# Expert stage of a mixture layer turned around: expert weights as the stationary operand, 96 token slots streaming past them

## The reference, cut to what matters

```python
logits = (h @ w_router).astype(jnp.float32)
top_val, top_idx = lax.top_k(logits, TOP_K)
top_w = jax.nn.softmax(top_val, axis=-1)
...
for e in range(N_EXPERTS):
    out = out + combine[..., e:e + 1] * _swiglu(h, w_gate[e], w_up[e], w_down[e])
```

## Time and profile before

| | |
|---|---|
| median of 3 runs | 1530.99 us (1530.94 to 2025.26) |
| profiled execution, first to last instruction | 1530.3 us |
| expert stage in it, from the first gather | 528.4 us to about 1520 us |
| one job | 123.2 us |
| PE, PEld busy | 1485.2 us (97%), 1268.3 us (83%) |
| DVE, ACT busy | 1154.3 us (75%), 1007.7 us (66%) |
| moved by DMA | 430.75 MB |

### The profile page before, as it was taken

How to read it: one execution, slowest core, us unless ns; L and a number is a source line. 1 busy time by engine, 2 the same in 40 slices (tenths; PEclk the granted TensorE clock), 3 DMA queues, 4 the chain that set the end, 5 groups by cost and what they waited for, 6 DMA issues and landing times.

```text
span 1530.3 us, 20635 instructions
## 1 busy us (share of the span) xinstructions
PE 1485.2 (97%) x7842; PEld 1268.3 (83%) x7842; DVE 1154.3 (75%) x872; ACT 1007.7 (66%) x834; POOL 15.5 (1%) x44
## 2 busy tenths in 40 slices
PE   5999999999999799999999999999999999999997
PEld 5898899997898688888888888888888888888775
DVE  4356644445456689888888888989889988888996
ACT  4568543344568477767767767777777777776775
POOL 3000000000000000000000000000000000000000
PEclk9999999999999899999999999999999999999998
DMA  9433455554433389999999989999999998998993
GB/s 342 139 115 109 165 180 179 178 192 154 149 125 111 124 305 372 370 326 376 377 319 373 373 323 373 375 336 355 373 370 326 375 374 317 375 376 320 351 368 119
DMA packets 185376, 430.75 MB, mean 281 GB/s; under 512 B 9048, under 2 KB 11096, under 8 KB 185328
## 3 DMA queue, kind: packets, MB, share of 16 engines
q1 hardware_dynamic: 181920, 426.27, 77.7%
q0 software_dynamic: 1184, 3.22, 0.7%
q10 hardware_dynamic: 2224, 0.59, 0.2%
HBM read 429.01 MB, written 1.05 MB: 281 GB/s over the span
## 4 chain that ended last, share of the span: by engine, by line
PE 89%; ACT 4%; DVE 3%; issue 2%; DMA 1%; ACTq 0%; DVEq 0%
PE ps L1264 81%; PE ps L1605 2%; PE ps L1635 2%; DMA wif<-in_w_in_dram 1%; ACT whi L454 1%; DVE wlo L835 1%; ACT L464 1%; PE ps L1411 1%; PE ps L1283 1%; DVE y L857 0%; PE ps L1672 0%; PE ps L1670 0%; PE ps L1424 0%; DVE y L1022 0%; ACT qkc L626 0%
## 5 line engine op out<-in xcount | busy, mean ns | idle before, releaser
L835 DVE TENSOR_TENSOR wlo<-raw,whi 128x2048 fp32r<-128x2048 f32 x405 | 926.4, 2291 | 294.3 <-ACT whi L454 293.9
L454 ACT ACTIVATE whi<-raw 128x2048 fp32r<-128x2048 f32 x405 | 776.8, 1919 | 409.2 <-PE ps L1264 408.3
L1264 PE MATMUL ps<-whi,xT_hi 128*128 128x512 f32 x1056 | 418.7, 397 | 1.5 <-DVE wlo L835 1.5
L1264 PE MATMUL ps<-wlo,xT_hi 128*128 128x512 f32 x1056 | 412.6, 391 | 0.0
L1264 PE MATMUL ps<-whi,xT_lo 128*128 128x512 f32 x1056 | 411.7, 390 | 0.0
L1264 PEld LDWEIGHTS ps<-wlo,xT_hi 128*128 128x128 f32 x1056 | 198.4, 188 | 42.5
L1264 PEld LDWEIGHTS ps<-whi,xT_hi 128*128 128x128 f32 x1056 | 198.9, 188 | 41.1 <-issue 1.7
L1264 PEld LDWEIGHTS ps<-whi,xT_lo 128*128 128x128 f32 x1056 | 199.1, 188 | 39.3
L1264 PE MATMUL ps<-whi,hid_hi 128*128 128x512 f32 (+1 forms) x536 | 210.9, 393 | 0.7 <-DVE hid_lo L1150 0.7
L1264 PE MATMUL ps<-wlo,hid_hi 128*128 128x512 f32 (+1 forms) x536 | 208.7, 389 | 0.0
L1264 PE MATMUL ps<-whi,hid_lo 128*128 128x512 f32 (+1 forms) x536 | 208.7, 389 | 0.0
(11 more groups left out here) (218 smaller groups left out, 854.9 us busy)
## 6 DMA issues: line engine op xcount, KB each, us to landing
raw<-in_moe_w_gate_dram SPq DMA_DIRECT2D x112, 1024.0 KB, 5.1
raw<-in_moe_w_up_dram SPq DMA_DIRECT2D x112, 1024.0 KB, 5.3
raw<-in_moe_w_down_dram SPq DMA_DIRECT2D x112, 1024.0 KB, 5.1
raw<-in_w_in_dram SPq DMA_DIRECT2D x28, 1024.0 KB, 5.2
raw<-in_ffn_w_gate_dram SPq DMA_DIRECT2D x10, 1024.0 KB, 5.2
raw<-in_ffn_w_up_dram SPq DMA_DIRECT2D x10, 1024.0 KB, 5.1
raw<-in_ffn_w_down_dram SPq DMA_DIRECT2D x10, 1024.0 KB, 4.9
raw<-in_w_out_dram SPq DMA_DIRECT2D x8, 1024.0 KB, 4.9
```

Of the source, the lines that this page charges most:

```text
L454: act.activation(whi[:, i % NSPLIT, :], raw[:, i % NRAW, :], ACT.Copy).then_inc(hi_ready, 1)
L835: dve.tensor_tensor(wlo[:, i % NSPLIT, :], raw[:, i % NRAW, :], whi[:, i % NSPLIT, :].bitcast(F32), ALU.subtract).then_inc(lo_ready, 1)
L1264: ins = pe.matmul(acc, lhs, rhs, start=start and m == 0, stop=stop and m == 2, skip_group_check=True)
```

## The change

What it does in the expert stage:

- Slots per job are 96 (CAP) and no longer 128; a second level of overflow is added (LEVELS = 2, EXTRA = 5: an expert with more than 96 tokens gets one extra job, with more than 192 two).
- Gate and up: the weights are the stationary operand, 128 x 128 at a time, and the tokens stream. High and low tokens stand side by side in `xg` (96 + 96 columns). For each of the 16 blocks of a piece there are two matmuls: the high weights with 192 columns, the low weights with the 96 high columns. The partial sums stand side by side too, and ACT (`rest`) and DVE (an add) join them. The result comes out transposed, so that `hid_transpose` and the split of the hidden values go.
- Down: plain float32, weights from `raw` as stationary operand, 96 columns of `hid_e` streaming, 16 matmuls for a piece; no split by ACT or DVE. The output comes out transposed (`outT`), 8 transposes turn it (`out_rows`).
- Buffers: `raw` has 9 slots, 7 in a ring for gate and up (NPIPE), 2 for down (NDOWN); splits run 4 ahead (NHALF). `qkc`, `om`, `vs`, `qsT`, `ksT` of the mixer now lie in slots 6 to 8.
- Issue order on SP: gate pieces of block f, down pieces of block f - 2, up pieces of block f.
- Ahead of the jobs: the four first splits all stand behind `norm_stats(3)` and `norm_rows(3, 5)`, none in the mixer's tail.

```diff
-            def product(i, bank, gathering=None):
-
+            def columns(s, m, gathering=None):
+
+                b = s // 4
+                if b:
+                    pe.wait_ge((gate_sum, up_sum)[m], loop.at("block", b))
                 for half in range(2):
                     if gathering is not None:
-
                         pe.wait_ge(xg_ready, loop.at("half", 2 * gathering + half + 1))
-                    hi, lo = piece(n + i + half, 4)
-                    for k in range(4):
-                        kk = 4 * half + k
-                        ins = passes(ps[:, bank, :], xT_hi[:, kk, 0:P], xT_lo[:, kk, 0:P],
-                                     hi[:, k, :], lo[:, k, :], start=half == 0 and k == 0,
-                                     stop=half == 1 and k == 3, weights_move=True)
+                    i = s + half
+                    pe.wait_ge(lo_ready, loop.at("piece", n + i + 1))
+                    hi, lo = (v[i % NHALF].rearrange("p (k n) -> p k n", k=4)
+                              for v in (half_hi, half_lo))
+                    for c in range(4):
+                        acc = ps[:, 2 * m + c // 2, 2 * CAP * (c % 2):2 * CAP * (c % 2) + 2 * CAP]
+                        cs = slice(c * P, (c + 1) * P)
+                        for k in range(4):
+                            x = xg[:, 4 * half + k]
+                            pe.matmul(acc, hi[:, k, cs], x.rearrange("p m n -> p (m n)"),
+                                      start=half == 0 and k == 0 and c % 2 == 0, stop=False,
+                                      skip_group_check=True)
+                            ins = pe.matmul(acc[:, CAP:], lo[:, k, cs], x[:, 0, :], start=False,
+                                            stop=half == 1 and k == 3, skip_group_check=True)
                     ins.then_inc(piece_used, 1)
...
             def down_job(f):
                 pe.wait_ge(e_hid, loop.at("block", f + 1))
-                down_piece_job(f, 0)
-                if f == EB - 2:
-                    hid_transpose(EB - 1)
-                down_piece_job(f, 1)
+                if f == 0:
+                    pe.wait_ge(tile0_done, loop.at("job", 1))
+                for half in range(2):
+                    pe.wait_ge(down_in[half], loop.at("down_in", 16 * (f + 1)))
+                    w = raw[:, NPIPE + half, :].rearrange("p (k n) -> p k n", k=2)
+                    for kk in range(2):
+                        for d in range(KC):
+                            ins = pe.matmul(ps[:, 6 + d // 4, CAP * (d % 4):CAP * (d % 4) + CAP],
+                                            w[:, kk, d * P:(d + 1) * P],
+                                            hid_e[:, f % 2, 2 * half + kk, :],
+                                            start=(f, half, kk, d % 4) == (0, 0, 0, 0),
+                                            stop=(f, half, kk) == (EB - 1, 1, 1),
+                                            skip_group_check=True)
+                    ins.then_inc(down_used, 1)
...
+            def out_rows():
+
+                pe.wait_ge(outT_ready, loop.at("job", 1))
+                for d in range(KC):
+                    ins = pe.transpose(ps[0:CAP, 4 + d // 4, (d % 4) * P:(d % 4) * P + P],
+                                       outT[:, d, :], ident[:])
+                ins.then_inc(o_ps, 1)
...
             def rest_of_job(then_next):
...
+                down_job(0)
+                for f in range(2, EB):
+                    columns(4 * f, 0)
+                    columns(4 * f + 2, 1)
                     down_job(f - 1)
-                if then_next:
+                if not then_next:
+                    down_job(EB - 1)
+                    out_rows()
+                    pe.wait_ge(scatT_ready, loop.at("job", 1))
+                    scatter(0)
+                    scatter(1)
+                else:
                     gather(1)
-                down_job(EB - 1)
-                if then_next:
-                    product(JOB_PIECES, 0, gathering=1)
-                scatter()
-                if then_next:
-                    scatter_matrix()
-                    product(JOB_PIECES + 2, 1)
+                    down_job(EB - 1)
+                    columns(JOB_SPLITS, 0, gathering=1)
+                    out_rows()
+                    columns(JOB_SPLITS + 2, 1)
+                    scatter(0)
+                    columns(JOB_SPLITS + 4, 0)
+                    scatter(1)
+                    columns(JOB_SPLITS + 6, 1)
+                    scatter_matrix(1)
```

On ACT, ahead of the router's copies and for the sums of a block (DVE's splits stand in the same way behind `norm_rows(3, 5)`):

```diff
             norm_stats(3)
-            split_upto(MOE_BASE + 2)
+            for s in range(NHALF):
+                act.wait_ge(gate_in[s], 16)
+                if s < NSPLIT:
+                    act.wait_ge(piece_used, MOE_BASE + s - NSPLIT + 1)
+                act.activation(half_hi[s], raw[:, s, :], ACT.Copy).then_inc(hi_ready, 1)
...
+            def rest(s, m, ready):
+
+                act.wait_ge(piece_used, loop.at("piece", n + s + 1))
+                b = s // 4
+                if b:
+                    act.wait_ge((gate_sum, up_sum)[m], loop.at("block", b))
+                act.activation(rest_e[:, m].rearrange("p (b c) n -> p b c n", b=2),
+                               sums(2 * m)[:, :, :, 1], ACT.Copy).then_inc(ready, 1)
```

More of the change, by code:

```diff
@@ L267, in trunk @@
         X_MIX, X_FFN, X_ROUTE = (0, 6), 4, 10
-        PER_JOB = {"piece": JOB_PIECES, "block": EB, "job": 1, "tile": TT, "half": 2}
+        PER_JOB = {"piece": JOB_SPLITS, "down": JOB_DOWNS, "block": EB, "job": 1, "tile": TT,
+                   "half": 2, "gate_in": 16 * JOB_SPLITS // NPIPE, "down_in": 16 * JOB_DOWNS // NDOWN}
         @block.sync
@@ L331, in _, with job @@
             mixer(1)
-            def job(e):
-                n = MOE_BASE
+            def job(e, first=False):
                 def expert(w):
                     return w[0, bass.ds(e, 1)].rearrange("e r c -> (e r) c")
-                for f in range(EB):
[L340 to L349, removed]
@@ L353, in _ @@
+                for f in range(EB):
+                    columns(f, gate, 0)
+                    if f >= 2:
+                        rows_down(f - 2)
+                    columns(f, up, 2)
+                rows_down(EB - 2)
+                rows_down(EB - 1)
+            loop.per = PER_JOB
+            job(0, first=True)
+            with sp.Fori(1, E) as j:
+                loop.reg = j
                 job(j)
             sp.wait_ge(table_ready, 1)
-            jobs = sp.value_load(table_i[0:1, 3:4], min_val=E, max_val=JOBS)
+            jobs = sp.value_load(table_i[0:1, EXTRA:EXTRA + 1], min_val=E, max_val=JOBS)
@@ L1247, in _ @@
                     one_hot(0)
-                    for i in range(NSPLIT):
-                        split(n + i)
+                    for s in range(NHALF):
+                        split_half(s)
                     start_of_job()
@@ L1677, in start_of_job, with scatter_matrix @@
+            def scatter_matrix(o):
+                pe.wait_ge(job_done, loop.at("job", 1 + o))
+                pe.wait_ge(xg_ready, loop.at("half", 2 * o + 2))
+                for t in range(TT):
+                    ins = pe.transpose(ps[0:CAP, 4, t * P:(t + 1) * P], slots[:, t, :], ident[:])
+                ins.then_inc(scatT_ps, 1)
             def start_of_job():
                 gather(0)
-                scatter_matrix()
-                product(0, 0, gathering=0)
-                product(2, 1)
@@ L1683, in rest_of_job @@
[L1683 to L1702 removed]
+                columns(0, 0, gathering=0)
```

445 lines of the change are left out of this document (250 added, 195 removed).

## The result

The changed kernel takes 2013.35 us (median of 4 runs, 2011.69 to 2013.52), the kernel before took 1531.68 us on the same chip: 1.315 times as long, 95% interval 1.313 to 1.317. The forecast was 1834 us with a range of 1775 to 1890. The direction was right; 303 us more were expected and 482 came. The ratio leaves out one run of the kernel before, which took 2025.26 us in a slower state of the chip. The profiled execution has a span of 2011.3 us and a mean granted clock of 0.939.

What follows compares the result with a forecast made beforehand. PE was taken as the bound, with DMA close behind. To 1530.3 us it added 290 for eight longer jobs, 9 ahead of the jobs and 4 of tail: 1833, or 1834 as the median of runs; range 1775 to 1890 us.

Steps and rivals of the forecast that it cites:

- What bounds the kernel before: Expert stage: PE is the bound, DMA close behind with a floor of 113.8 us a job; work off other engines worth nothing.
- Gate and up, 115 ns a step: Gate and up matmuls: full weight load sets the step, 110 to 120 ns, including 7 for fp32r; 103.0 us a job.
- Down, 110 ns a record: Down matmuls in plain float32: 32 records a piece at 110 ns, 49.3 us a job where fp32r passes took 38.1.
- The job, 159.5 us of work: One expert job on PE: all steps summed, 36.3 us more than 123.2; times eight, +290 us (+254 to +326).
- I cost all this at 0, with 10 us over the whole stage as the upper end: Expert stage: new waits for sums, splits, hidden products and SP's down slots are hidden; 0, at most 10 us.
- clock 1.00 from the first columns on: Expected sign in the profile after: PE at full clock from the first columns of the expert jobs.
- The clock falls: Rival, expert stage: at 1.2 GHz steps take about 215 ns, a job about 296 us, 2900 us in all; chance 0.05.
- Loads hide: Rival, PE's matmuls: only columns count, 80 + 13 and 40 + 13 ns in gate and up; 1468 us; chance 0.04.
- fp32r loses its rate below 256 columns: Rival, gate and up: short fp32r matmuls take four cycles a column, as plain float32; 2823 us; chance 0.09.
- The cover for the sums: Gate and up: PE returns to its banks after 7.4 us, ACT and DVE need 5.2; at 73 ns steps PE would wait.
- Ahead of the jobs, 9 us: Before the expert jobs: four splits ahead of router copies and pick, router at half clock; pick 9 us later (3 to 12).
- Tail, 4 us more: After the last down matmul: copying sums, transposes, whole-row splits and scatter add some 4 us, 2 to 6.

Runs made afterwards that it cites:

- the kernel with no long waits: Changed kernel with SP issuing the next job's first gate and up pieces before the last two down pieces, PE's job loop written out: 1837.32 us, ratio 1.200.
- 64 slots: Kernel with SP's earlier issue and PE's jobs written out, streaming only 64 of 96 slots, tokens in the others left out: 2850.47 us, clock 0.607.
- another: Changed kernel with ACT and DVE finishing a job's last block before splitting the next job's first four pieces: 1959.42 us, ratio 1.281.

## Why the prediction was right and wrong

- **What bounds the kernel before**, and that only PE's steps count: right. Removing half of the load of gate and up took 260 us off at once, and the kernel with no long waits sits on 8 x PE's work.
- **Gate and up, 115 ns a step** (110 to 120): measured 111.6. The lower end was nearer: the 7 ns of fp32r do not come on top once the load is the longer side.
- **Down, 110 ns a record:** measured 111.4. Plain float32 does cost more than three split passes here, 49.9 us for 38.1.
- **The job, 159.5 us of work:** 157 (156.7 by the one job without half clock), but 186.4 from gather to gather. The failed step is the one that put the new waits at nothing: "I cost all this at 0, with 10 us over the whole stage as the upper end". They and the half clock behind them cost 205. Its argument about SP ("two down and two up pieces are 10.8 us of transfer, and PE has the block of 14.7 us in between") holds inside a job, where PE has no wait row. I never walked through the job's end, where two blocks of down pieces follow one another on SP's queue and the next job's gate pieces stand behind them. I named what is queued behind SP's wait, and did not ask who waits for that: ACT, which has the last block's steps behind the split.
- **The clock:** "clock 1.00 from the first columns on" was wrong, since in the changed kernel each wait is followed by a stretch at 1.2 GHz, about 6 us a job. The rival "The clock falls" with its 215 ns steps and 2900 us did not come with 96 slots, but it came, nearly to the number, with 64 (213 ns, 2850 us). It was a better rival than its 0.05, though the number is near in part by luck: its forecast was for 96 slots.
- **The rival "Loads hide"** is out at full loads (223 ns a pair, not 146), and the same arithmetic of columns is what holds with loads of 64. **"fp32r loses its rate below 256 columns"** is out: 96 and 192 columns in 223 ns. Its "four cycles a column" for plain float32 was misread in any case: the rows with 128 columns (109 ns a record) are no dearer than those with 8 (110), so they show the load and not the columns.
- **The cover for the sums:** right that it was enough, wrong that 73 ns a step would be too fast for it. With loads of 64 columns the steps are 73 ns apart, and the view of PE's waits has no row ahead of gate and up.
- **Ahead of the jobs, 9 us:** 5. The row of the pick's first step shows it, against 521.29; the router's 32 records took 7.00 us at half clock, as forecast, so what was too large was the delay of their start. ACT began its four splits at 511.49 us and not at 514.80, where its one split had stood before, because the norm ahead of them no longer stood behind a split of the mixer's tail.

```profile
519.32 7.00 PE L1688 MATMUL ps<-wr,raw 128*128 128x8 f32 x32 [4.86 <-ACT raw L773]
...
526.35 0.24 DVE L1167 COPY rt<-ps 128x8 f32<-128x8 f32 x2 [4.00 <-PE ps L1688]
```

- **Tail, 4 us more:** right. The last of 64 down records that begin at 1984.83 us starts at about 1991.85 (63 x 111.4 ns later), and DVE's add 6.8 us behind it, against 2.66.

```profile
1998.66 1.28 DVE L1277 SCALAR_TENSOR_TENSOR h<-ps,job_w,h 128x1024 f32<-128x1024 f32 x1 [2.09 <-PE ps L1777]
```

No version that does the whole work beats the kernel before: the best is 1837 us, and with every wait gone the stage still has 157 us of PE work a job for 123.

## What to carry to other kernels

Count matmuls by their weight loads as well as by their columns, and take the longer of the two: a full float32 or fp32r load cost 112 ns a step here, so fewer streamed columns gave nothing. When a change puts two kinds of transfer on one queue, walk through the seam of the loop, not only its steady state, and follow the first transfer of the next round through each in-order engine back to the work of this round. If PE waits once in a round, price the stretch at half clock behind it too; it can be several times the wait, and it need not be the same at every seam.

## What the runs showed of the hardware that I had not expected

- The granted clock fell to 1.2 GHz while PE was busy without a gap (64 slots, 1112 to 1116 us), and stayed there for hundreds of microseconds of back-to-back matmuls with few columns beside full loads. With 192 and 96 columns it came back, after 4 us in one kernel and 14 in another, but in that other one only after 58 and 65 us at two of seven seams.
- Streaming fewer tokens made the kernel slower by 1044 us (3057.85 for 2013.35).
- PE lost 3.1 to 3.8 us a round behind the jump back of a loop whose body is a whole job, and the view of waits put it down to an engine that had nothing to do with it.
- A step with a full load costs 111.6 ns at full and 213 ns at half clock, whatever it streams between 64 and 192 columns.
